# One decoder step in fp32: state updates among dense tiles, two first tiles in other banks, wide output weights with the MLP's first sums ahead, two products in the third bank, last rows in halves

## What is computed

```python
hn = rmsnorm(h, norm_mix)
z, xbc, dt_raw, q, k, v = split(hn @ w_in)         # 1024 x 4112
y_ssd, new_conv, new_ssm = ssd_branch(z, xbc, dt_raw, conv_state, ssm_state, ...)
y_att = moba_attention(q, k_all, v_all, q_start, rel_bias)
h = h + concatenate([y_ssd, y_att]) @ w_out
h = h + cross_attend(rmsnorm(h, norm_ca), mem_k, mem_v, w_ca_q, w_ca_o)
hn = rmsnorm(h, norm_mlp)
h = h + square(relu(hn @ w_up)) @ w_down           # 1024 x 4096 and back
y = rmsnorm(h, norm_final)
```

## Time and profile before

| | |
|---|---|
| device time, median of 3 runs | 665.31 us (664.91 to 666.43) |
| the profiled execution | 667.34 us, span 665.7 us |
| TensorE busy | 636.7 us |
| TensorE weight loads (beside the products) | 508.4 us |
| VectorE, ScalarE, GpSimd busy | 405.3, 154.1, 137.9 us |
| moved by DMA | 125.75 MB, 189 GB/s over the span |
| mean granted TensorE clock | 0.99 of full speed |

### The profile page before, as it was taken

One profiled execution on the slowest core, in us unless ns is written; L12 is line 12 of the kernel. 1 busy time (PEld: TensorE's weight loads), 2 busy tenths in 40 slices (PEclk: granted clock), 3 DMA queues, 4 the chain that ended last, 5 costly groups with the idle time before them and its releaser, 6 DMA issues.

```text
span 665.7 us, 13151 instructions
## 1 busy us (share of the span) xinstructions
PE 636.7 (96%) x4891; PEld 508.4 (76%) x4891; DVE 405.3 (61%) x878; ACT 154.1 (23%) x410; POOL 137.9 (21%) x221
## 2 busy tenths in 40 slices
PE   9899999999999999989999998989999999999994
PEld 7666776676675755456657875789999999999994
DVE  2475577997654665695432344689787883644733
ACT  3210020010223774682202333221111110000001
POOL 6242112210300025051001100315444350000000
PEclk9999999999999989999999999999999999999997
DMA  8898878898831169675686631635445454544501
GB/s 294 249 301 279 272 255 267 278 295 249 237 99 56 64 210 305 237 189 166 194 278 224 230 132 59 212 105 175 143 152 166 136 182 159 179 139 139 177 3 71
DMA packets 100459, 125.75 MB, mean 189 GB/s; under 512 B 6459, under 2 KB 78671, under 8 KB 100402
## 3 DMA queue, kind: packets, MB, share of 16 engines
q1 hardware_dynamic: 94754, 106.81, 49.9%
q0 software_dynamic: 5648, 18.14, 8.6%
HBM read 116.63 MB, written 8.31 MB: 188 GB/s over the span
## 4 chain that ended last, share of the span: by engine, by line
PE 69%; DVE 7%; SPq 2%; issue 2%; ACT 1%; POOL 1%; DMA 1%; DVEq 0%; POOLq 0%; ACTq 0%
PE ps L1583 32%; PE ps L1170 22%; PE ps L1129 3%; PE ps L1235 2%; PE ps L1401 2%; PE ps L1188 1%; SPq L825 1%; PE ps L1347 1%; SPq L827 1%; POOL acc L984 1%; PE ps L1135 1%; DMA big<-in_cache_v 1%; PE ps L1277 1%; DVE rstd L2141 1%; PE ps L1476 1%
## 5 line engine op out<-in xcount | busy, mean ns | idle before, releaser
L1170 PE MATMUL ps<-hw,wring 128*128 128x288 f32 x576 | 147.8, 412 | 1.5 <-DVE qs L2083 1.4
L1170 PEld LDWEIGHTS ps<-hw,wring 128*128 128x128 f32 x576 | 108.0, 191 | 37.1 <-issue 5.8
L2218 DVE STREAM_TRANSPOSE tmp<-big 128x1024 f32<-128x1024 f32 x32 | 37.9, 1222 | 3.3 <-PE ps L1188 3.2
L1583 PE MATMUL ps<-hw,wring 128*128 128x144 f32 x256 | 34.2, 287 | 1.1 <-DVE hw L2069 1.1
L984 POOL TENSOR_TENSOR acc<-acc,sq 128x288 f32<-128x288 f32 (+1 forms) x35 | 28.1, 804 | 29.7 <-ACT sq L1806 27.2
L1583 PE MATMUL ps<-big,wring 128*128 128x144 f32 x256 | 34.0, 286 | 0.0
L1583 PEld LDWEIGHTS ps<-hw,wring 128*128 128x128 f32 x256 | 32.5, 190 | 1.6 <-DVE hw L2069 1.6
L2065 DVE COPY tmp<-ps 128x512 f32<-128x512 f32 (+6 forms) x34 | 20.8, 617 | 20.8 <-PE ps L1129 15.8
L1170 PE MATMUL ps<-attT,wring 128*128 128x288 f32 x128 | 32.0, 407 | 1.4 <-DVE attT L2065 0.8
L1170 PE MATMUL ps<-big,wring 128*128 128x288 f32 x128 | 32.7, 408 | 0.0
L1583 PEld LDWEIGHTS ps<-big,wring 128*128 128x128 f32 x256 | 32.4, 190 | 0.0
(11 more groups left out here) (343 smaller groups left out, 1157.5 us busy)
## 6 DMA issues: line engine op xcount, KB each, us to landing
wring<-in_w_in SPq DMA_DIRECT2D x16, 1024.0 KB, 7.2
wring<-in_w_up SPq DMA_DIRECT2D x16, 1024.0 KB, 5.0
wring<-in_w_down SPq DMA_DIRECT2D x16, 1024.0 KB, 4.8
big<-in_cache_v SPq DMA_DIRECT2D x56, 256.0 KB, 3.3
big<-in_cache_k SPq DMA_DIRECT2D x36, 256.0 KB, 3.6
big<-in_cache_k POOLq DMA_DIRECT2D x28, 256.0 KB, 4.2
wring<-in_w_ca_kv SPq DMA_DIRECT2D x4, 1024.0 KB, 8.1
big<-in_state_ssm SPq DMA_DIRECT2D x8, 512.0 KB, 6.4
```

What stands on the lines that cost most here:

```text
L1170: last = pe.matmul(ps[:, BANK[key], 0:width], w, rhs, start=(k == 0), stop=(k == K_TILES[kind] - 1))
L1583: last = pe.matmul(ps[:, bank_, col * HALF:(col + 1) * HALF], w(k), x(k), start=(start and k == 0), stop=(stop and k == 3))
L2218: dve.transpose(KT_[:, step_ % 2].rearrange("p c (w j) -> p w c j", j=32), src[:, :, :, m, :])\
```

## The change

The edits, in the order of the run:

- **Entry.** 12 warm products instead of 18. The first two tiles (`qk` 0) go to banks 4 and 5, so that the third tile does not follow them in bank 0; the first key page waits for their eviction. The second tile stands ahead of the norm's sum, the fourth memory transpose ahead of the replication of q (`qrep`). ScalarE reads every norm's sum from PSUM in the square root itself, with scale and eps; the copy is gone.
- **Updates.** Decays and updates start one tile sooner, among the last `z` tile and the `v` tiles, in groups of 2, 2, 3, 3, 3, 3 instead of 2, 3, 4, 7. The bank order is `UP_BANK`: banks 4 and 5 twice, then 7, 4, 5. The reads in bank 7 are taken by a step of its own (`ysr`, `sample_reads`: two copies and two adds) behind `stt`.
- **Cross heads.** `head_bound("cross", 2)` moves behind the copies of `probs` 3; the evicting engines of `probs` 2 and 3 are named.
- **Output tiles.** Weights of `oa` and `cao` come in blocks of 512 columns (`WIDE`), one slot for four tiles, with four key tiles of 512 in place of four of 256 in a slot; the tile program waits for each pair of head results ahead of the product that reads them and not ahead of the tile. Each freed slot goes to an MLP chunk at once (`load_up`, within the walk through the list). Chunk 0's weight sums are made ahead of the first cross output tile, chunk 1's one at a time behind the first four of them, the activation sums in parts behind tiles 5, 6 and 7 (`early_sums`).
- **Products.** The product of the fourth weight sum moves from bank B to bank C, ahead of the last one, and the semaphore for bank B is given one product sooner. `products` only returns the views; `up_chunk` and `down_pair` now write their own adds, as many as before, in an order in which bank C is read last.
- **End.** The two row blocks are scaled and stored in halves of 512 columns, four transfers of 256 KB instead of two of 512.

The core of the diff:

```diff
 UP_BANKS = [4, 5, 7]
-WARM = 18
+UP_BANK = [4, 5, 4, 5] + [7, 4, 5] * 4
+WARM = 12
...
     item("vec")
+    tile("qk", 0, 1)
     item("ss", "x")
-    tile("qk", 0, 1)
...
+    item("memt", 3)
     item("qrep")
-    item("memt", 3)
...
     item("stt")
+    item("ysr")
+    item("decay", 0, 4)
+    item("upd", 0, 2)
...
-    item("decay", 0, 12)
-    item("upd", 0, 2)
+    item("decay", 4, 16)
+    item("upd", 2, 4)
     tile("v", 0, 0)
     item("ys")
-    item("upd", 2, 5)
+    item("upd", 4, 7)
     tile("v", 0, 1)
-    item("upd", 5, 9)
+    item("upd", 7, 10)
+    tile("v", 1, 0)
+    item("upd", 10, 13)
     item("tok", 0)
-    item("decay", 12, 16)
-    tile("v", 1, 0)
-    item("upd", 9, 16)
+    item("upd", 13, 16)
...
 SEQ = make_plan()
+WIDE = ("oa", "cao")
...
+BLOCKS, LAST_TILE = [], {}
 for s in SEQ:
     if s[0] == "tile":
-        if s[3] == 0:
-            BLOCK[s[1:3]] = len(BLOCK)
+        if s[3] == 0 and s[1] in WIDE and s[2] % 2:
+            BLOCK[s[1:3]] = BLOCK[(s[1], s[2] - 1)]
+        elif s[3] == 0:
+            BLOCK[s[1:3]] = len(BLOCKS)
+            BLOCKS.append(s[1:3])
+        LAST_TILE[BLOCK[s[1:3]]] = s[1:4]
...
-N_BLOCKS, N_TILES = len(BLOCK), len(TILE)
+N_BLOCKS, N_TILES = len(BLOCKS), len(TILE)
...
 for t in TILE:
-    BANK[t] = len(BANK) % 2
+    BANK[t] = 4 + t[2] if t[:2] == ("qk", 0) else len(BANK) % 2
...
         elif s[0] == "ss":
-            turn(s)
+            turn(s, "act"), FREELY.add(s)
...
         elif s[0] == "probs":
-            turn(("probs", s[1], 0))
+            if s[1] < 2:
+                turn(("probs", s[1], 0))
+            else:
+                turn(("probs", s[1], 0), "dve" if s[1] == 2 else "act"), FREELY.add(("probs", s[1], 0))
...
+            k, width = K_TILES[kind], 512 if kind in WIDE else 256
...
                 k = K_TILES[key[0]]
-                sp.dma_start(wring[:, g % SLOTS, 0:k * 256].rearrange("p (k n) -> p k n", k=k),
+                sp.dma_start(wring[:, g % SLOTS, :].rearrange("p (k n) -> p k n", k=k),
...
+            def load_up(n):
+                s = chunk_slot(n)
+                sp.dma_start(wring[:, s, :].rearrange("p (k n) -> p k n", k=DT),
+                             up[:, 256 * n:256 * n + 256].rearrange("(k p) n -> p k n", p=P)).then_inc(landed[s], 16)
             for s in SEQ:
-                if s[0] == "tile" and s[3] == 1:
+                if s[0] == "tile" and s[1:] == LAST_TILE[BLOCK[s[1:3]]]:
...
+                    else:
+                        sp.wait_ge(dense_ps, TILE[s[1:]] + 1)
+                        load_up(g + SLOTS - N_BLOCKS)
...
                     load_unit(UNIT[s[1:]] + 2)
...
+            for n in range(SLOTS, N_UP):
+                chunk_done(sp, n - SLOTS)
...
                         .then_inc(fnorm_in, 16)
...
+            for i in range(2):
+                cols = slice(512 * i, 512 * i + 512)
+                sp.wait_ge(y_dve, i + 1)
+                sp.dma_start(O["y_prompt"][0:P, cols], yrow[0][:, cols]).then_inc(y_out, 16)
+                sp.wait_ge(y_act, i + 1)
+                sp.dma_start(O["y_prompt"][P:2 * P, cols], yrow[1][:, cols]).then_inc(y_out, 16)
+            sp.wait_ge(y_dve, 3)
             sp.dma_start(O["y_sample"], yrow[2][0:NS, :]).then_inc(y_out, 16)
...
                 block_ready(pe, (kind, n))
...
+                wide, col = kind in WIDE, half * P + (256 * (n % 2) if kind in WIDE else 0)
                 for k in range(K_TILES[kind]):
+                    if first and kind == "oa":
+                        if k == 0:
+                            turned(pe, ("ohead", 1))
+                        turned(pe, ("pv", "self", 2 * k)), turned(pe, ("pv", "self", 2 * k + 1))
+                    elif first and kind == "cao":
+                        if k == 0:
+                            pe.wait_ge(scores_used, 4)
+                            turned(pe, ("ohead", 3))
+                        turned(pe, ("pv", "cross", k))
...
                         rhs, width = hw[:, k, :], T
...
                         turned(pe, IN_SCORES[0])
+                        tile_done(pe, ("qk", 0, 1))
...
                 r = NS * (2 * g + bh)
-                if k == 2:
-                    pe.wait_ge(ys_made, 1)
-                if k >= 3:
-                    pe.wait_ge(up_done, k - 2)
-                pe.matmul(ps[:, UP_BANKS[k % 3], :], xwt[r:r + NS, j * P:(j + 1) * P], bbd[r:r + NS, :],
+                if k == 4:
+                    pe.wait_ge(reads_taken, 1)
+                elif k >= 2:
+                    pe.wait_ge(up_done, k - 1 if k < 4 else k - 2)
+                pe.matmul(ps[:, UP_BANK[k], :], xwt[r:r + NS, j * P:(j + 1) * P], bbd[r:r + NS, :],
...
                 pe.wait_ge(hs_made, 2)
-                product(B, 1, summed(n, 2), x_sum(2), True, True)
-                product(B, 2, summed(n, 3), odd_late, True, True).then_inc(dense_ps, 1)
+                product(B, 1, summed(n, 2), x_sum(2), True, True).then_inc(dense_ps, 1)
+                product(C, 1, summed(n, 3), odd_late, True, True)
...
                     product(B, 0, summed(n, 0), x_sum(0), begin, False)
-                    product(B, 1, summed(n, 2), x_sum(2), False, False)
-                    last = product(B, 2, summed(n, 3), odd_late, False, end)
+                    last = product(B, 1, summed(n, 2), x_sum(2), False, end)
                     if end:
                         last.then_inc(dense_ps, 1)
-                    product(C, 0, raw(n, 1, 1), x_sum(3), begin, end).then_inc(dense_ps if end else chunk_used, 1)
+                    product(C, 1, summed(n, 3), odd_late, begin, False)
+                    product(C, 0, raw(n, 1, 1), x_sum(3), False, end).then_inc(dense_ps if end else chunk_used, 1)
...
                     if NORM[key[1]]:
-                        act.wait_ge(root_done, NORM[key[1]])
-                    act.activation(vv[:, 0:n], ps[:, bank(key), 0:n], ACT.Copy, scale=1.0 / D).then_inc(turn_act, 1)
+                        act.wait_ge(rstd_done, NORM[key[1]])
+                    act.activation(rmem[:, :] if key[1] == "mem" else rstd[:, :], ps[:, bank(key), 0:n], ACT.Sqrt,
+                                   bias=eps_t[:, 0:1], scale=1.0 / D).then_inc(turn_act, 1)
...
                     last.then_inc(turn_dve, 1)
-                    return
...
+            def sample_reads():
+                dve.wait_ge(ssT_used, 16)
+                dve.wait_ge(cv_out, 32)
+                halves = [yo[:, g * 512:(g + 1) * 512] for g in range(2)]
+                for g in range(2):
+                    last = dve.tensor_copy(halves[g], ps[32 * g:32 * g + 32, 7, :])
+                step(last)
+                for g in range(2):
+                    last = dve.tensor_tensor(halves[g], ps[64 + 32 * g:96 + 32 * g, 7, :], halves[g], ALU.add)
+                last.then_inc(reads_taken, 1)
...
+            def weight_sum(n, i):
+                w = wring[:, chunk_slot(n), :].rearrange("p (k o h n) -> p k o h n", k=4, o=2, h=2)
+                t = w_sums[n % 2]
+                y, x_, op = ((w[:, :, 0, 1], w[:, :, 1, 1], ALU.add), (t[:, 0], w[:, :, 0, 0], ALU.subtract),
+                             (w[:, :, 0, 0], w[:, :, 0, 1], ALU.subtract), (w[:, :, 1, 0], t[:, 1], ALU.subtract))[i]
+                ins = dve.tensor_tensor(t[:, i], y, x_, op)
+                if i == 3:
+                    ins.then_inc(ws_made, 1)
+                elif i < 2:
+                    step(ins)
...
-            def activation_sums():
-                x = hw[:, :, :].rearrange("p (k o) t -> p k o t", o=2)
+            def activation_sum(i, lo, hi):
+                x = hw[:, :, :].rearrange("p (k o) t -> p k o t", o=2)[:, lo:hi]
                 a, b = (x[:, :, 0, 0:HALF], x[:, :, 0, HALF:T]), (x[:, :, 1, 0:HALF], x[:, :, 1, HALF:T])
...
+                t = [h[:, lo:hi, :] for h in hw_sums]
+                y, x_ = ((a[1], a[0]), (b[1], t[0]), (b[1], a[1]), (b[0], t[1]))[i]
+                return dve.tensor_tensor(t[i], y, x_, ALU.subtract)
+            def early_sums(c):
+                if c < 4:
+                    if c == 0:
+                        chunk_ready(dve, 1)
+                    weight_sum(1, c)
+                elif c == 5:
+                    dve.wait_ge(hw_done, 16 + 6)
+                    rows_stored(dve)
+                    step(activation_sum(0, 0, 3))
+                    step(activation_sum(1, 0, 3))
+                elif c == 6:
+                    dve.wait_ge(hw_done, 16 + 7)
+                    activation_sum(2, 0, 3)
+                    activation_sum(3, 0, 3)
+                    step(activation_sum(0, 3, 4))
+                elif c == 7:
+                    dve.wait_ge(hw_done, 16 + 8)
+                    activation_sum(1, 3, 4).then_inc(hs_made, 1)
+                    dve.wait_ge(hs_made, 1)
+                    activation_sum(2, 3, 4)
+                    activation_sum(3, 3, 4).then_inc(hs_made, 1)
...
                 if s[0] == "tile":
```

(49 more changed lines are left out.)

98 lines of the change are left out of this document (18 added, 80 removed).

## The result

The changed kernel takes 658.78 us (median of four executions: 657.90, 657.94, 659.61, 659.89), the kernel before beside it 665.57. The ratio is 0.9895 (95% interval 0.9879 to 0.9911). A second set of four, beside the experiments, gave 657.61 and 0.9875 (0.9856 to 0.9894). The forecast was 654.0 with a range of 651.0 to 658.5: right in its sign, too large by 4.8 us, and 0.3 outside its range.

The account below looks back on a forecast made before the run. TensorE, busy 96% of the span, was taken as the bound, so only its waits, low-clock stretches and ends could pay. Terms -1.5 - 4.2 - 0.9 - 3.5 - 0.9 - 0.3 = -11.3 us took 665.31 to 654.0; range 651 to 658.5.

Parts of the forecast that it names:

- Entry: Start of the kernel, to the tile behind the replication: -1.5 us, bounds 0 and -3.0.
- almost the same: Norm chain at the entry: the reciprocal would end at 22.6, where it ended at 22.92 before.
- Rival 4: First tiles: with 12 warm products TensorE stays at 1.2 GHz, 4.08 us more per tile, about 670; chance 0.03.
- Updates: State updates among the tiles: -2.1 from new groups and -2.1 from keeping the clock, together -4.2 us.
- Rival 1: Between the last two v tiles the clock falls again, giving back 2.1: 656.1 us; chance 0.14.
- What comes behind the updates: After the updates: no term of its own in the sum; the updates were said to bring no new wait.
- K pages or V pages that are hidden now: Sign of a wrong forecast in the profile after: waits for these pages; no size or chance given.
- Cross probabilities: Cross heads: the wait for eviction of the sample probabilities goes once the third head's bound stands behind the copy; -0.9 us.
- Output tiles and MLP entrance: Last head's values to chunk 1's third product: 5.0 us of waits go, 1.5 (0.9 and 0.6) come back; -3.5.
- Rival 2: Output tiles: VectorE becomes the bound as early weight sums meet GpSimd adds; gain 1.5 instead of 3.5, 656.0; chance 0.09.
- Third bank: End of the MLP: bank B's signal 0.98 earlier lets the final transposes start near 656.8 instead of 657.65; -0.9 us.
- Rows in halves: Last rows: the first half can be issued 0.3 us sooner; -0.3 us, bounds +0.4 and -0.4.

Follow-up runs that it names:

- e1_kv_later: Changed kernel with the transposes of the 32 sample tokens' keys and values moved from ahead of tok 1's to behind outputs 0 of block 1; 654.98 us, 0.9844.
- e4_norm_alone: Kernel before with one edit alone: ScalarE takes each norm's square root straight from PSUM, without the copy; 662.59 us, 0.9951.
- e2_old_entry: e1_kv_later with the entry as before (18 warm products, old banks and order), keeping the one-step square root; 654.20 us, 0.9815.
- e3_entry_mixed: e2_old_entry with the fourth memory transpose ahead of the replication of q, as in the change; 656.60 us, 0.9861.
- e2_bank_b: e1_kv_later with the fourth weight sum's product back in bank B and VectorE's adds in the matching order; 657.07 us, 0.9861.
- e4_old_updates_kv: Changed kernel with decays and updates in old places and groups, and sample tokens' key and value transposes moved as in e1_kv_later; 661.18 us, 0.9934.
- e2_late_sums: e1_kv_later with chunk 0's weight sums ahead of the seventh cross output tile, activation sums then chunk 1's weight sums behind the last; 655.58 us, 0.9851.
- e1_same: Changed kernel run again without any edit, beside the other runs; 657.61 us, 0.9875.

## Where the prediction failed, and where it held

By its own steps, each against the profiles:

- **Entry, predicted -1.5.** Wrong in its working, and near only in executions whose first tile keeps the clock. In the recorded profile -0.14, without the clock's drop -2.0 (e1_kv_later). What failed is what follows from "almost the same". For the changed order that sentence is right where the first tile keeps the clock: the reciprocal ends at 22.03 in e1_kv_later (23.85 in the recorded profile), before at 22.92. But it is so because the second tile ahead of the sum eats the 1.7 of the copy and the table load, and I looked for the gain in the banks and not there. The one-step square root alone gives the 1.6 (e4_norm_alone); banks, order and 12 warm products add 0.3 at best (34.55 in e1_kv_later, 34.88 in e2_old_entry, but 34.14 in e4_norm_alone, which has none of them), and the fourth memory transpose ahead of the replication takes 0.85 (e3_entry_mixed). The two waits that I foresaw, 1.0 and 1.5, are there with 1.63 each.
- **The clock in the first tile.** Rival 4 had it in a harsher form (all first tiles, 670). It lasts one tile and costs 1.7. It drops in the three profiles where TensorE waited 0.55 to 0.89 for the weights, and in none of the others of this entry, with at most 0.25 of wait. The same three are those whose 24 warm records ended soonest (4.43 to 4.79 us, the others 4.89 to 5.49), and no run keeps the two apart. With 18 warm products there is no such wait, and the first tile takes 4.15 in all six profiles. The prediction found the weights at about 11 and the transposes' end ahead of that, and did not price the gap.
- **The other norms, predicted 0.** The same edit gives 0.75 at the memory's norm and 1.24 at the MLP's (below). I had followed it at one of its five places only.
- **Updates, predicted -4.2.** Right: -4.6 in the profile, 2.3 of it in the sums and the last v tile at full clock and 2.3 in the groups, no clock drop in that execution. (A decay is four ScalarE instructions, 48 records for twelve, and not three; the times counted here were those of the rows.) Rival 1 holds for four of the 13 profiles with the new order (the last v tile takes 5.52 to 5.70), while the last v tile of all four profiles with the old order (before among them) takes 5.16 to 5.24. The Trainium skill ("TensorE: Matmul & The Clock Gate", "A second HAM failure mode: psum-queue depth-cycling") says that short stalls between groups are enough for a drop; the traces agree in that nothing in that stretch waits longer than 0.19 us when it happens, but the nine other profiles have the same small wait and keep the clock. What decides between the executions no run here shows.
- **What comes behind the updates, predicted 0.** This is the step that failed: +3.3 us. I looked for the waits of TensorE that the updates held back and did not ask which transfers had been hidden by them. The store of the keys goes into a stretch where the DMA engines are full (share 0.93 to 1.03 from 250 to 268 before). Issued 5.5 us sooner it lands only 1.7 sooner, and VectorE's next write into `sq`, now ready 6.0 us sooner (at 261.4, before 267.45), waits 4.04 us for it: 2.6 us of wait on TensorE and 0.7 at the lower clock. e2_bank_b and e4_old_updates_kv show that it is this wait, and that the updates' gain brings it out. The prediction named "K pages or V pages that are hidden now" as what would prove it wrong, but gave it no price and no chance, and it was a store.
- **Cross probabilities, -0.9:** 0.65; a remainder of 0.28 stays.
- **Output tiles and MLP entrance, -3.5:** 3.4, and the single wait that is left, 1.62 ahead of chunk 0's second product, is about the 0.9 and the 0.6 that I gave back. Beside GpSimd's adds two of the activation sums took 1.08 and 1.20 us where their like take 0.61, in the recorded profile and in e1_kv_later. But the reasons are shared out otherwise. Only 0.9 belongs to the early sums (e2_late_sums), 1.0 to the wait that now stands inside the first output tile, and 1.2 to 1.5 to the reciprocal, which waits for ScalarE and stood ahead of chunk 1's sums; the one-step norm removes that wait alone (e4_norm_alone). Rival 2 did not come: where the early weight sums met GpSimd's adds (at 415.4, 416.9 and 418.7) they kept their 0.68, and GpSimd's adds took 1.10 instead of 0.79.
- **Third bank, -0.9:** 0.82 in the profile, 0.6 undone. **Rows in halves, -0.3:** 0.2.
- **The signs and the range.** Held: no wait ahead of the third tile, clock 1.00 through 240 to 256, the last v tile 5.5 us sooner, 0.61 ahead of the final transposes. Not held: the tile behind the replication at 35 (36.38), chunk 1's third product 10 us sooner (6.6), no low clock between 20 and 650 (0.58 at 268 to 271). The lower end of the range does not follow from its own rule: half of the excess of the best bounds is 1.3 us, which gives 652.7; all of it gives 651.4.

That e2_old_entry measures 654.2, next to the forecast of 654.0, is in part luck: its entry gains the 1.5 that I had promised, but by the one edit that I had held to change nearly nothing there, and the memory's norm adds 0.8 that I had not counted.

## What to carry to other kernels

A stage that gets faster issues its stores sooner into the same full DMA queues: for each buffer that is written again, compare issue to landing with the distance to the next write, as it will be. An edit in a helper acts at every place that calls it; price each. What an engine waits for is often decided by one operation ahead in another engine's queue (a reciprocal, a copy), so change its place first, and other banks and buffers after that.

## What the runs showed of the hardware

- The granted clock drops for about one tile, and whether it does differs between executions of one kernel: it costs 1.4 to 1.7 us each time. The two executions of the changed kernel near 659.7 have a mean clock of 0.991, those at 657.9 one of 0.994, and 654.98 us of e1_kv_later 0.997.
- After an idle time of 2.58 us the granted clock was 0.58 over the 3 us from 268 to 271, after 2.15 us in e1_same 0.50: in the first case the stretch lost 3.3 us in all, 0.7 more than the wait.
- A store's time from issue to landing is not its own: the same 256 KB took 6.6 us before and 10.4 us in the changed kernel, with the DMA engines' share near 1.0 in both.
- The moment from which the warm products are fast varies: 24 records took 4.43 to 5.49 us, 36 records 6.32 to 7.07. So the first tile starts up to 0.75 us sooner or later for the same code. In half-microsecond windows the count of records rises from 4 or 5 to 6 or 7 at 4.5 us in the recorded profile of the changed kernel and at 7.0 in that of before, while the granted-clock column reads 1.00 all along: that column does not show the slow start. The prediction's sentence by the Trainium skill ("TensorE: Matmul & The Clock Gate", "What's actually happening"), that fewer warm products put the transposes at the lower clock, is not borne out: the 24 transposes take 4.41 us behind 12 warm products and behind 18, also in e2_late_sums, where all 24 warm records were slow (5.49 us). They take 0.18 us each, and later ones of the same size 0.13 (twelve in 1.53 at 204.01 in the profile before), so something other than the clock may set their pace; no run shows which.
